# Gated DeltaNet stage of a hybrid trunk: the triangular inverse from substituted 16x16 blocks, decay rows by DMA, and the output norm in the next head

## The reference

```python
qkv = silu(centred_conv(h @ w_qkv));  q, k = l2norm(q) * 128**-0.5, l2norm(k)
gc    = cumsum(g) in the chunk;  decay = exp(where(i >= j, gc_i - gc_j, NEG))
a_mat = where(i > j, beta_i * (k_i . k_j) * decay, 0) + I
u, w  = solve(a_mat, v * beta),  solve(a_mat, k * beta * exp(gc))    # unit triangular
qk    = (q . k) * decay
# scan over the chunks, once forward and once backward:
v_new = u - w S;   o = (q * exp(gc)) S + qk v_new;   S = S * g_last + kd^T v_new
o     = rmsnorm(o_f + o_b, o_norm) * silu(z)
```

## Time and profile before

| | us |
|---|---|
| median of 3 runs | 4103.93 (4100.78 to 4105.41) |
| profiled execution, device time | 4102.51 |
| its span (first to last instruction) | 4100.7 |
| PE busy | 3672.0 (90%) |
| DVE busy | 2175.1 (53%) |
| POOL busy | 1087.5 (27%) |
| ACT busy | 1038.2 (25%) |
| mean granted TensorE clock | 0.960 of 2.4 GHz |

### The profile page before, as it was taken

The page is one execution under the profiler, slowest core; times in us unless marked ns, Lnnn a source line. Parts: engine busy times, 40 slices in busy tenths (PEclk is TensorE's granted clock), DMA queues, the critical chain, the costliest instruction groups (busy, mean ns, idle before and its releaser), DMA issues. The chain is left out here.

```text
span 4100.7 us, 58018 instructions
## 1 busy us (share of the span) xinstructions
PE 3672.0 (90%) x23042; PEld 3523.5 (86%) x23042; DVE 2175.1 (53%) x2921; ACT 1038.2 (25%) x1411; POOL 1087.5 (27%) x645
## 2 busy tenths in 40 slices
PE   4973998999999996898989899898989899999996
PEld 3961787999999995888888888888989799999996
DVE  7758546533434456657566575757565522322226
ACT  3135422111111113323333332423331311111110
POOL 2223003211111112424252333324253312111121
PEclk8986999999999997999999999999999999999998
DMA  4420101212112111000000000000002011111111
GB/s 173 163 78 18 41 23 60 84 64 84 63 62 83 62 57 74 18 13 19 25 6 30 2 29 8 24 13 18 30 33 83 31 42 42 47 42 42 42 42 67
DMA packets 58875, 198.61 MB, mean 48 GB/s; under 512 B 6768, under 2 KB 18288, under 8 KB 57712
## 3 DMA queue, kind: packets, MB, share of 16 engines
q1 hardware_dynamic: 58608, 194.72, 13.4%
HBM read 179.95 MB, written 14.75 MB: 47 GB/s over the span
## 5 line engine op out<-in xcount | busy, mean ns | idle before, releaser
L55 PE MATMUL psum<-h_high,panel_high 128*128 128x384 f32 x3624 | 1240.1, 342 | 102.4 <-DVE h_low L495 78.3
L56 PE MATMUL psum<-h_low,panel_high 128*128 128x384 f32 x3624 | 1222.1, 337 | 0.0
L57 PE MATMUL psum<-h_high,panel_low 128*128 128x384 f32 x3624 | 1221.6, 337 | 0.0
L187 POOL TENSOR_TENSOR panel_low<-panel_raw,panel_high 128x1024 fp32r<-128x1024 f32 x196 | 486.7, 2483 | 2253.2 <-ACT panel_high L182 2207.9
L55 PEld LDWEIGHTS psum<-h_high,panel_high 128*128 128x128 f32 x3624 | 688.8, 190 | 123.4 <-issue 72.2
L56 PEld LDWEIGHTS psum<-h_low,panel_high 128*128 128x128 f32 x3624 | 689.6, 190 | 0.3
L57 PEld LDWEIGHTS psum<-h_high,panel_low 128*128 128x128 f32 x3624 | 688.6, 190 | 0.0
L847 DVE TENSOR_TENSOR ffn_product<-ffn_silu_gate,psum 128x1152 f32<-128x1152 f32 x44 | 59.6, 1354 | 711.4 <-PE psum L57 710.0
L55 PE MATMUL psum<-ffn_mid_high,panel_high 128*128 128x384 f32 x1056 | 356.0, 337 | 14.7 <-DVE ffn_product L847 7.8
L182 ACT ACTIVATE panel_high<-panel_raw 128x1024 fp32r<-128x1024 f32 x195 | 205.3, 1053 | 619.9 <-PE psum L57 560.1
L57 PE MATMUL psum<-ffn_mid_high,panel_low 128*128 128x384 f32 x1056 | 354.7, 336 | 0.0
(11 more groups left out here) (302 smaller groups left out, 5622.6 us busy)
## 6 DMA issues: line engine op xcount, KB each, us to landing
panel_raw<-in_stream SPq DMA_DIRECT2D x197, 512.0 KB, 3.3
ffn_mod_panels<-in_wmod SPq DMA_DIRECT2D x24, 1024.0 KB, 7.5
in_mod_panels<-in_wmod SPq DMA_DIRECT2D x16, 1024.0 KB, 5.4
first_mod_panels<-in_wmod SPq DMA_DIRECT2D x8, 1024.0 KB, 14.0
x<-in_x SPq DMA_DIRECT2D x3, 1536.0 KB, 14.4
x<-in_x SPq DMA_DIRECT2D x1, 4608.0 KB, 16.4
x_spill<-x SPq DMA_DIRECT2D x1, 4608.0 KB, 12.9
x<-x_spill SPq DMA_DIRECT2D x1, 4608.0 KB, 13.8
```

The lines of the kernel that those rows point to most:

```text
L55: pe.matmul(out, wh, xh, start=first, stop=False)
L56: pe.matmul(out, wh, xl, start=False, stop=False)
L57: return pe.matmul(out, wl, xh, start=False, stop=last)
L187: pool.tensor_tensor(self.wl[buf][:], self.raw[buf][:], self.wh[buf][:].bitcast(F32), ALU.subtract).then_inc(self.split_low.sem, 1)
```

## The change

- **Inverse.** `LEVELS` becomes [16, 32, 64]: 9 slots a direction. The diagonal 16x16 blocks are inverted before by substitution. SP writes the diagonal blocks of `wt` to DRAM (8 DMAs of 16 partitions x 9 x 16 elements a direction), waits for them, and reads them back so that each partition holds the whole 16x16 block of its group, for all nine chunks (`rep`, 9216 bytes a partition). Then 31 small elementwise steps, each waiting for the one before it, give the inverse block (`substitute`): d = 0 on DVE, d = 1 on POOL. `expand` (DVE) spreads it into `tt`; PE turns `tt` in three groups (`turn_of`) and ACT copies them (`turned`).
- **Decay rows.** The sums are transposed once in `decay_stage` and stored in DRAM; each head loads four row tiles by a broadcast DMA of 128 x 9 x 128: two for the exponents (into `qn` and `v_tok`), two already exponentiated for `qg`. The 18 matmuls against `tri` and their evacuations are gone. POOL does the subtraction and the mask, for the next head, during the scan (`exponents`); ACT takes exp.
- **wt.** ACT scales kk by beta as it leaves PSUM, 18 copies of 128x128; DVE multiplies by the decay. `kg` moves from POOL to ACT in the same form.
- **Output norm.** Square, sum, root, reciprocal, product and gate of head h now stand in head h+1: the sum after PE's panel 2, the DVE steps (`finish_o`) after `expand(0)`. In the last head they stay at the end.
- **Order.** The convolutions of q and v leave the levels and stand before and behind the substitution. q's norm moves from the levels of d = 1 to those of d = 0. k.k stands behind the first third of panel 2. Head 0 stands apart, heads 1 to 6 are the loop.

```diff
-LEVELS = [2, 4, 8, 16, 32, 64]
+BASE = 16
+LEVELS = [16, 32, 64]
...
+        def substitute(eng, d, h):
...
+            eng.wait_ge(rep_full[d], 16 * h + 16)
...
+            eng.tensor_tensor(inv[:], unit, unit, ALU.mult).then_inc(sub_step[d], 1)
+            for i in range(BASE - 1):
...
+                n = BASE - 1 - i
+                eng.wait_ge(sub_step[d], step + (2 * i + 1))
+                eng.tensor_tensor(part[:, :, 0:n], rep[:, :, m, cols], inv[:, :, m:m + 1].to_broadcast([P, NT, n]),
+                                  ALU.mult).then_inc(sub_step[d], 1)
+                eng.wait_ge(sub_step[d], step + (2 * i + 2))
+                eng.tensor_tensor(inv[:, :, cols], inv[:, :, cols], part[:, :, 0:n], ALU.subtract
+                                  ).then_inc(sub_step[d], 1)
...
+                for d in range(2):
+                    sp.wait_ge(wt_ready, 2 * h + (d + 1))
+                    for b in range(NK):
+                        lines = slice(b * BASE, (b + 1) * BASE)
+                        sp.dma_start(s.blocks_dram[d, b].rearrange("n m c -> m n c"),
+                                     by_block(dn.wt[d])[lines, :, lines]).then_inc(a_out, 16)
+                    sp.wait_ge(a_out, 32 * NK * h + 16 * NK * (d + 1))
+                    sp.dma_start(dn.rep[d][:].rearrange("p n m c -> p (n m c)"),
+                                 s.blocks_dram[d].rearrange("b (o n) m c -> b o (n m c)", o=1
+                                                            ).to_broadcast([NK, BASE, NT * BASE * BASE])
+                                 ).then_inc(rep_full[d], 16)
...
+                    sp.wait_ge(qg_ready, 2 * h + 2)
+                    sp.wait_ge(u_full, 2 * h + 2)
+                    for d in range(2):
+                        rows(h + 1, d, dn.rows[d]).then_inc(rows_full, 16)
```

More of the change, by code:

```diff
@@ L1835, in body @@
+                masked(0, 1)
                 split(h, 4)
[L1836 to L1849 removed]
+                substitute(pool, 1, h)
@@ L1850, in body @@
+                for c in range(2, SLOTS):
+                    masked(0, c)
+                for c in range(SLOTS):
+                    masked(1, c)
+                    if c == 1:
+                        decayed_q(0)
+                    if c == 3:
+                        decayed_q(1)
+                    if c == 5:
+                        kd(0)
+                if more:
+                    split(h, 5)
+                kd(1)
                 decayed()
                 if more:
+                    exponents(h + 1)
@@ L2094, in _, with body @@
             norm_k(1)
-            def body(h, more):
+            def body(h, first, more):
                 def full(n):
@@ L2126, in body, with scaled, turned @@
-                split(h, 3)
-                full(FULL_R0)
-                take(dn.qg[0], 1, ACT.Exp)
+                def scaled(out, src, q, d, n):
+                    return act.activation(blk(out, n), src, ACT.Copy, scale=dn.hs[:, q, d, n:n + 1])
+                def turned(d, g):
+                    use = use_of_turn(d, g)
+                    act.wait_ge(xb_full, USES * h + (use + 1))
+                    act.activation(dn.t[d][:, g * TW:(g + 1) * TW], psum[:, 6 + use % 2, 0:TW], ACT.Copy
+                                   ).then_inc(xb_read, 1)
@@ new lines, in x_copy @@
+                def x_copy(d, c):
+                    n, use = SLOTS * d + c, use_of_x(d, c)
+                    act.wait_ge(xb_full, USES * h + (use + 1))
+                    if n >= 2:
+                        act.wait_ge(d_full, 2 * SLOTS * h + (n - 1))
+                    act.activation(dn.xl[n % 2], psum[:, 6 + use % 2, 0:TW], ACT.Copy).then_inc(xb_read, 1)
+                split(h, 3)
+                for d in range(2):
+                    act.wait_ge(dec_ready, 2 * h + (d + 1))
+                    act.activation(dn.pt[d][:], dn.rows[d][:], ACT.Exp).then_inc(decay_act, 1)
@@ new lines, in body @@
+                if not first:
+                    act.wait_ge(decay_act, 4 * h + 2)
+                    square_o(h)
+                act.wait_ge(head_ready, h + 1)
+                full(FULL_KK)
+                for d in range(2):
+                    for n in range(NT):
+                        a = scaled(dn.wt[d], psum[:, 3 + n // 3, (n % 3) * P:(n % 3 + 1) * P], BETA_, d, n)
+                    a.then_inc(decay_act, 1)
+                act.wait_ge(decay_act, 4 * h + 4)
+                act.sem_inc(grp_read, 1)
@@ L2243, in _, with body @@
             norm_k(1)
-            decay(0, 0)
-            def body(h, more):
+            def body(h, first, more):
                 def norm_q(t):
```

529 lines of the change are left out of this document (283 added, 246 removed).

## The result

The changed kernel takes 4007.75 us (median of 4 runs, 4001.56 to 4018.73) against 4104.22 beside it: ratio 0.977, 95% interval 0.975 to 0.979. It is faster, by 96 us; the forecast was 257 (3847) with a range up to 3945. The sign was right, the size and the range were wrong. The profiled execution has a span of 4017.0 us.

A forecast was written before the change was run, and what follows sets the result against it. PE, busy 90% of the span, was taken as the bound. Its work falls 40.2 us a head, new waits leave 32 gained: 8 x 32 = 256 off 4102.5, plus 1.4, gives 3847; range 3785 to 3945 (8 in 10).

The forecast's parts named there:

- 1 k ready: Before k.k: DVE's reciprocal starts about 1 us sooner, k ready 7.35 and 1.36 us later; PE idles 6 us.
- 2 `wt` of d = 0: k.k on PE 2.1 us, nine scaled copies on ACT 1.7, product with the decay on DVE 1.4.
- 3 `rep` of d = 0: Eight block writes, 3.6 us to issue and 3.0 to land, then the read-back of 1152 KB, 6.1 with its issue.
- 4 substitution, `expand`: On DVE after the read-back: 31 dependent steps in 8.3 us, then `expand` 1.4.
- 5 `finish_o`, v's convolution: On DVE before its first update: output norm 11.6 us, v's convolution 7.9; PE waits for it.
- 6 levels of d = 0: Levels of d = 0, bound by DVE's updates, `expand(1)` and q's norm: 21.2 us.
- 7 `decayed_q`, mask: On POOL after q's norm: `decayed_q`, 2.63 us, ahead of the third mask of d = 1, 0.91.
- the slow read-back: Read-back on 8 engines at half rate: 4.7 us a head, 38 in all, 3885; chance 0.18.
- POOL's half: Substitution of d = 1 on POOL: 14.5 us, done at 1875.5, needed by DVE at 1885.3; taken as hidden.
- the third rival: POOL's half takes 25 to 32 us or more, `expand(1)` waits; at 32, 64 us in all, 3911; chance 0.15.
- the second rival: Same as the slow read-back: half rate on 8 engines, 38 us in all, 3885; chance 0.18.
- The slower rival: Block writes land one after another at 5 us each, POOL's half 57 us late: 4303; chance 0.05.

The follow-up runs named there:

- e6: The changed kernel with each read-back taking 128 different 9216-byte pieces from the weights in one DMA, inverse blocks zero: 3893.8 us, one run.
- e10: The changed kernel with read-backs taking different pieces from the weights, eight in the source's slowest dimension, inverse blocks zero: 4010.3 us, one run.
- e11: The changed kernel with the two loads for the scaled q issued behind the second read-back instead of before the first block writes: 3996.9 us.
- e8: The changed kernel with the second third of panel 2 ahead of k.k on PE instead of behind it: 4006.5 us.
- e3: The changed kernel with each read-back split into eight DMAs of 144 KB, one for each group of 16 partitions: 3990.9 us.
- e9: e3 with the eight pieces 64 KB apart in DRAM instead of 9 KB: 3990.8 us.
- e7: The changed kernel with all block writes first, output norm before substitution, read-backs in two parts, and scaled q's loads after the read-backs: 3931.2 us.

## Why the prediction was wrong, step by step

Times are us after the sum of k's squares, in the second head; the forecast's axis less 1823.7, the changed kernel's less 1817.6.

| step | forecast | measured | added by the step |
|---|---|---|---|
| 1 k ready | 12.3 | 12.3 | 0 |
| 2 `wt` of d = 0 | 17.5 | 20.5 | +3.0 |
| 3 `rep` of d = 0 | 30.2 | 43.2 | +10.0 |
| 4 substitution, `expand` | 39.9 | 52.9 | 0 |
| 5 `finish_o`, v's convolution | 59.4 | 69.3 | -3.1 |
| 6 levels of d = 0 | 80.6 | 100.2 | +9.7 |
| 7 `decayed_q`, mask | 84.1 | 103.9 | +0.2 |
| 8 PE's tail, to q.k | 98.7 | 121.2 | +2.7 |
| POOL: `rep` of d = 1 | 37.3 | 57.4 | |
| POOL: steps done | 51.8 | 75.2 | |

- **The step that failed first is 3**, the cost of the writes and of the read-back. The read-back took 12.9 us and not 6.1, and e6 prices it: with a load that lands in 5.4 us, 114 of the 161 us come back (one run). I had its cost from the earlier trace rows, from two groups of loads of distinct data; the same list has 24 loads of 1024 KB at 7.5 us and eight at 14.0, which I left out. I had given the slow read-back 0.18 at 4.7 us a head. Its mechanism was right, and "DMA: Bandwidth & Descriptors" of the Trainium skill, section "Why a DMA increments its semaphore by 16 and not by 1", agrees with the trace: half of the engines, 0.51 busy. Its price was too small: it halved the rate, where the rate fell by 2.5 (277 GB/s in e6, 110 here and 112 in e10), and it counted DVE's side only. The writes took 9.8 us and not 6.6, 5.0 of it behind qg's loads (e11), which I had put beside the scan at 3.5 us each; they land after 14.4. For d = 1 they took 13.7, behind the first read-back, over the 10 us that I had named as a sign of a wrong mechanism.
- **POOL's half is the second.** Its forecast hung on the same number twice: its writes queue behind the first read-back, then its own read-back follows. It began 20.1 us late and took 17.8 us instead of 14.5. What the third rival foretold came, PE waiting for the third mask, but not for its reason: it wanted 24 us or more for the steps. The lateness came with the read-back, so the second rival and the third share a cause, and I had added them up as alternatives. Where POOL's steps stretch, DVE has an instruction with two SBUF inputs, as "SBUF — State Buffer" of the Trainium skill, section "Who interferes with whom", says; the rows at 1878.0 and 1879.6 agree. One other, 0.80 us at 1881.06, lies beside a TENSOR_SCALAR with one tensor input (1880.67 to 1881.60). The reciprocal, on which I had counted, did protect the first six steps.
- **Step 6** follows from it: PE waits 6.42 us for the third mask and works at half clock behind it. In e6, where that wait is gone, the stretch from the first update to the last piece of q's norm took 21.8 us (21.2 forecast for the step) instead of 30.4, so the step's own sum was right.
- **Step 2** was a clock term: k.k took 4.18 us, not 2.1, after the idle time that step 1 forecast correctly, and the eighteen scaled copies 4.76 us instead of 3.4. I had allowed 1 us a head for all effects of the clock, where there are 2.1 at k.k and up to 2.7 in the tail. Its worth on the path stays open (e8).
- **Steps 1, 4, 5 and 7 held**: k at 12.3, 31 steps in 8.4 us (8.3), 3.7 for qg and mask (3.54). Step 5 was 3 us too long in the forecast, since I took durations from beside long instructions of POOL, and here only its short steps lie there. The last sum, 3846.5 + 1.4, gives 3847.9 and not 3847, which changes nothing.
- **The range** added one rival at a time to the forecast. The terms share a cause, so the bad case is their sum: 22.5 us in this head, about 20 on average, 161 in all.
- **The slower rival** did not come: eight writes overlap and take 4.8 us undisturbed (e11), not 40.

## What to carry to other kernels

Before costing a DMA by its size, ask how many engines its shape gives it, whether the loads from which you take the price had the same form, and what is queued ahead of it; a wrong size enters once for every read-back queued behind another. When a new chain replaces work on a busy engine, follow both of its ends to the first instruction that needs either, and look at what stands in one queue ahead of a short, urgent operation. Here moving POOL's products (2.6 and 2.1 us) behind two or three more of its 0.9 us masks was worth 52 us, more than any edit of the DMAs that keeps the result. Rivals that share a cause are added, not chosen between.

## What the runs showed of the hardware

- A load of 1152 KB in pieces of 9216 bytes: 277 GB/s in the window as one DMA of 128 different pieces (e6), 113 with all engines busy as eight DMAs, each filling sixteen neighbouring partitions with one piece (e3); 416 and 1066 ns a piece. 64 KB between the pieces of the latter changes nothing (e9). Which of the differences matters isn't shown.
- On half of the engines a piece takes 611 to 629 ns, shared or not (e10, the changed kernel), longer than the 416 on all of them.
- Two issues of loads took SP 13.69 us while read-backs were moving (e7), where two had taken 1.64 us (the changed kernel).
- Eight writes of 9 KB in runs of 64 bytes took 4.8 us from the first issue to the last landing with nothing ahead of them (e11), 9.8 behind two loads of 576 KB and 13.7 behind the read-back.
- POOL's dependent steps with 117 to 135 elements a partition take 0.4 to 0.5 us, DVE's 0.3; the former grow to 1.5 beside DVE instructions with two SBUF inputs.
